# Hybrid pooling and stick-breaking trunk on one core: the z and gate strips of the input projection by seven block products instead of eight

## What is computed

```python
def reference(x, norm_g, w_in, b_gate, pool_w, pool_scale, w_pool_up, w_attn_up, w_out, final_g):
    ...
        h = rms_norm(x, norm_g[l])
        proj = jnp.einsum('bsd,de->bse', h, w_in[l])
        u_pool, z_pool, q, k, v, z_attn, gate_logits = jnp.split(proj, splits, axis=-1)
        y_pool = multiscale_pool(u_pool, pool_w[l], pool_scale[l]) * jax.nn.silu(z_pool)
        attn = stick_breaking_attention(...)
        y_attn = attn.reshape(B, S, ATTN_WIDTH) * jax.nn.silu(z_attn)
        gates = jax.nn.sigmoid(gate_logits + b_gate[l]).reshape(B, S, 2, D)
        merged = (gates[:, :, 0] * jnp.einsum('bsp,pd->bsd', y_pool, w_pool_up[l])
                  + gates[:, :, 1] * jnp.einsum('bsa,ad->bsd', y_attn, w_attn_up[l]))
        x = x + jnp.einsum('bsd,de->bse', merged, w_out[l])
    return rms_norm(x, final_g)
```

## Time and profile before

| | |
|---|---|
| three runs, median | 1686.95 us (1686.09 to 1690.57) |
| the profiled execution | 1688.91 us |
| its span (first to last instruction) | 1687.1 us |
| PE busy | 1649.3 us (98%), 8306 matmuls |
| DVE busy | 930.7 us (55%) |
| ACT busy | 689.8 us (41%) |
| POOL busy | 550.8 us (33%), 468 instructions |
| DMA | 170.16 MB, 31.9% of 16 engines |
| mean granted clock of PE | 0.995 |

### The profile page before, as it was taken

The page is one execution under the profiler, slowest core; times in us unless marked ns, Lnnn a source line. Parts: engine busy times, 40 slices in busy tenths (PEclk is TensorE's granted clock), DMA queues, the critical chain, the costliest instruction groups (busy, mean ns, idle before and its releaser), DMA issues. The chain is left out here.

```text
span 1687.1 us, 25908 instructions
## 1 busy us (share of the span) xinstructions
PE 1649.3 (98%) x8306; PEld 1374.1 (81%) x8306; DVE 930.7 (55%) x1311; ACT 689.8 (41%) x1335; POOL 550.8 (33%) x468
## 2 busy tenths in 40 slices
PE   8999999998999999999999999999999899999998
PEld 6878888886888888888878888888888678888886
DVE  6736410004776678766767666777666674333423
ACT  4422221114555565555545555655555441111111
POOL 3531111115343354342443433543411341414040
PEclk9999999999999999999999999999999999999999
DMA  7621131222332232222313322322213573535331
GB/s 251 230 102 50 63 106 69 75 90 72 101 94 63 67 88 85 73 76 70 95 51 99 94 64 67 88 83 74 76 54 119 178 234 121 153 112 162 112 99 75
DMA packets 119930, 170.16 MB, mean 101 GB/s; under 512 B 44401, under 2 KB 61297, under 8 KB 119810
## 3 DMA queue, kind: packets, MB, share of 16 engines
q1 hardware_dynamic: 119810, 168.68, 31.9%
HBM read 114.11 MB, written 54.53 MB: 100 GB/s over the span
## 5 line engine op out<-in xcount | busy, mean ns | idle before, releaser
L1295 DVE TENSOR_TENSOR_SCAN left<-keep,left 128x512 f32<-128x512 f32 x192 | 285.2, 1485 | 119.7 <-ACT keep L1199 96.4
L1091 PE MATMUL psum<-hT_hi,w_parts 128*128 128x512 f32 x760 | 312.5, 411 | 1.3 <-POOLq L1424 1.3
L1093 PE MATMUL psum<-hT_lo,w_parts 128*128 128x512 f32 x760 | 307.5, 405 | 0.0
L1095 PE MATMUL psum<-hT_hi,w_parts 128*128 128x512 f32 x760 | 307.0, 404 | 0.0
L1199 ACT ACTIVATE keep<-psum 128x512 f32<-128x512 f32 (+3 forms) x320 | 170.9, 534 | 233.7 <-PE psum L1110 231.2
L1292 DVE TENSOR_TENSOR_SCAN left<-keep,floor 128x512 f32<-128x512 f32 (+3 forms) x128 | 112.4, 878 | 224.6 <-ACT keep L1199 223.6
L1206 ACT ACTIVATE wt<-psum 128x512 fp32r<-128x512 f32 (+3 forms) x320 | 170.7, 533 | 159.6 <-PE psum L1119 157.0
L1347 POOL TENSOR_TENSOR y_out<-row_sum 64x128 f32<-64x128 f32 x128 | 76.5, 598 | 398.5 <-DVE row_sum L1311 393.0
L1301 DVE TENSOR_TENSOR wt<-psum,wt 128x512 fp32r<-128x512 f32 (+3 forms) x320 | 192.1, 600 | 21.3 <-ACT wt L1206 14.4
L1130 PEld LDWEIGHTS psum<-wt,vm 128*128 128x128 f32 x1088 | 169.6, 188 | 34.1 <-DVE wt L1301 6.9
L1130 PE MATMUL psum<-wt,vm 128*128 128x256 f32 x1088 | 182.5, 282 | 3.0 <-DVE wt L1301 2.8
(11 more groups left out here) (123 smaller groups left out, 2644.7 us busy)
## 6 DMA issues: line engine op xcount, KB each, us to landing
w_raw<-in_w_strips SPq DMA_DIRECT2D x36, 512.0 KB, 4.2
gate_scratch<-staging SPq DMA_DIRECT2D x64, 256.0 KB, 2.5
gate<-gate_scratch SPq DMA_DIRECT2D x64, 256.0 KB, 4.0
xt<-in_x SPq DMA_DIRECT2D x16, 512.0 KB, 5.1
xT<-in_x_T SPq DMA_DIRECT2D x16, 512.0 KB, 4.1
qk_scratch<-staging SPq DMA_DIRECT2D x32, 256.0 KB, 2.4
k_raw<-qk_scratch SPq DMA_DIRECT2D x64, 128.0 KB, 3.3
q_raw<-qk_scratch SPq DMA_DIRECT2D x128, 64.0 KB, 2.6
```

Source lines behind the costliest of these rows:

```text
L1091: pe.matmul(o, hi, hT_hi[:, kt, tok], start=kt == 0, stop=False)
L1093: pe.matmul(o, hi, hT_lo[:, kt, tok], start=False, stop=False)
L1095: last = pe.matmul(o, lo, hT_hi[:, kt, tok], start=False, stop=kt == KT - 1)
L1295: dve.tensor_tensor_scan(left[:, n % 4, span][:, ::-1], k, k, carry, ALU.mult, ALU.bypass).then_inc(scanned, 1)
```

## The change

Take two strips (rows A1, A2 of a 2x2 block matrix, with K cut in two halves of 512: A11, A12, A21, A22) and two chunks of tokens (B11, B12, B21, B22). Four strip products are eight products of blocks, 12 matmuls each. The change makes them from **seven** block products by sums of blocks (Winograd's form): S3 = A11 - A21, S2 = A22 - S3, S1 = S2 + A11, S4 = A12 - S2 of the weights, and T1 = B12 - B11, T3 = B22 - B12, T2 = B22 - T1, T4 = B21 - T2 of the tokens; the seven products are summed into four results.

- **Groups.** 24 groups of two strips by two chunks (1024 tokens), in two phases: first all strips for the first 1024 tokens, then all for the other 1024. Group 0 stays plain (4 strip products; the first of them is now strip z 0 by chunk 1, at the end of stage 2); the other 23 have 7 products of 12 matmuls. The filler of stage 3 goes from 95 x 24 = 2280 matmuls to 3 x 24 + 23 x 84 = 2004.
- **Weights.** For each group POOL forms four sums of blocks (128x512) and splits off seven low halves (128x512, `ring`, five places); ACT makes the seven high halves.
- **Sums of products.** For each group ACT copies two products from PSUM (`take`), DVE adds five (`add_part`, line 1581 of the changed kernel), POOL adds two pairs in SBUF (`join`). The z groups' product with the sigmoid (`silu`) now reads its strip from SBUF.
- **Token sums.** Eight (T1 to T4 for each phase, with their parts) are made in stage 2 by DVE (80 additions of 128x512), ACT (32 high parts) and POOL (32 low parts), and stored to DRAM (`form_d`); the first phase's are loaded at the end of stage 2 and the opening of stage 3, the second phase's, with B11, B21 and B22, as 28 DMAs of 512 KB around the middle of stage 3, one to a step.
- **Written out.** Stage 3's loop over the two middle pairs is gone: all 320 steps are written out on every engine. `hT` is one tensor by blocks. Some of stage 4's tiles lie elsewhere.

```diff
+HK = KT // 2
+FORMS = 7
+B11, B21, T2, T1, T3, B22, T4 = range(FORMS)
+A11, A12, S2, S1, S3, S4, A22 = range(FORMS)
+HOME = {B11: 0, B21: 1, B22: 3, T2: 4, T1: 5, T3: 6, T4: 7}
...
 # stage2, SP
+            def put_t(v):
+                f, kk, i = t_unit(v)
+                sp.wait_ge(t_lo_done, v + 1)
+                sp.dma_start(form_d[f, TURN[i], kk], t_parts[:, i, :, :].bitcast(F32)).then_inc(t_stored[i], DMA)
+            def load_t(j):
+                for kk in range(HK):
+                    sp.dma_start(hT[:, HOME[j], kk, :, :].bitcast(F32), form_d[0, j, kk]).then_inc(form_in[j], DMA)
...
 # stage2, DVE
+            for f in range(2):
+                b11, b21, b12, b22 = range(4 * f, 4 * f + 4)
+                for kk in range(HK):
...
+                    dve.tensor_tensor(t_rest[:, 0, :], lo[2], lo[0], ALU.subtract).then_inc(t_step, 1)
+                    dve.tensor_tensor(t_rest[:, 1, :], lo[3], lo[2], ALU.subtract).then_inc(t_step, 1)
+                    dve.tensor_tensor(t1, hi[2], hi[0], ALU.subtract).then_inc(t_step, 1)
...
 # stage3
-    STRIPS = 6
-    GROUPS = STRIPS * NC
-    MM = 3 * KT
+    GROUPS = 6 * PAIRS
+    MM = 3 * KT
+    PART = 3 * HK
+    PLAIN = 4
...
+    cost = [450.0 + 3.1 * item(n)[3] for n in range(ALL)]
+    SWITCH = part(GROUPS // 2 - 1, 0)
+    calm = range(ALL // 2 - 14, ALL // 2 + 18)
+    cost = [x * (0.8 if s in calm else 1.0) for s, x in enumerate(cost)]
...
+    AHEAD_OF = (3, 3, 4, 4, 5, 5, 5)
+    def split_step(w):
+        return max(fin[freed(w)], fin[PLAIN + w - AHEAD_OF[w % FORMS]]) + 1
...
 # stage3, PE
-        with eng.Fori(1, PAIRS - 1) as p:
-            walk(p, range(NI), True, True, True)
+            def form_part(g, j):
+                w = split(g, j)
...
+                pe.wait_ge(w_lo_done, w + 1)
+                if g == 1 and j in (T1, T2, T3, T4):
+                    pe.wait_ge(form_in[j], HK * DMA)
+                if g == GROUPS // 2:
+                    pe.wait_ge(form_in[j], (2 if j in (T1, T2, T3, T4) else 1) * HK * DMA)
...
 # stage3, ACT
+            def take(g, j):
...
+                act.activation((sum_a if j == A11 else sum_c)[:, :], bank_p(part(g, j)), ACT.Copy).then_inc(taken, 1)
...
 # stage3, DVE
+            def add_part(g, j):
+                dve.wait_ge(part_done, part(g, j) + 1)
...
+                elif j == S3:
+                    dve.wait_ge(joined, 2 * (g - 1) + 1)
+                    dve.wait_ge(summed, 5 * (g - 1) + 2)
...
+                dve.tensor_tensor(to[:, :], bank_p(part(g, j)), a[:, :], ALU.add).then_inc(summed, 1)
...
 # stage3, POOL
+            def low_w(w):
+                g, j = w // FORMS + 1, w % FORMS
+                if j == A11:
...
+                    step(blocks[S3][:, :, :], blocks[A11][:, :, :], blocks[S3][:, :, :], ALU.subtract,
+                         w_formed, 4 * (g - 1) + 1)
...
+                    step(blocks[S2][:, :, :], blocks[A22][:, :, :], blocks[S3][:, :, :], ALU.subtract,
+                         w_formed, 4 * (g - 1) + 2)
+                pool.wait_ge(w_hi_done, w + 1)
+                step(ring[:, w % RING, 1, :, :], blocks[j][:, :, :], ring[:, w % RING, 0, :, :].bitcast(F32),
+                     ALU.subtract, w_lo_done, w + 1)
+                if j == A11:
+                    step(blocks[S1][:, :, :], blocks[S2][:, :, :], blocks[A11][:, :, :], ALU.add,
+                         w_formed, 4 * (g - 1) + 3)
+                if j == A12:
+                    step(blocks[S4][:, :, :], blocks[A12][:, :, :], blocks[S2][:, :, :], ALU.subtract,
+                         w_formed, 4 * (g - 1) + 4)
+            def join(g, j):
+                if j == S1:
...
+                    step(sum_b[:, :], sum_a[:, :], sum_c[:, :], ALU.add, joined, 2 * (g - 1) + 1)
+                else:
+                    pool.wait_ge(summed, 5 * (g - 1) + 3)
+                    step(sum_c[:, :], sum_a[:, :], sum_c[:, :], ALU.add, joined, 2 * (g - 1) + 2)
```

More of the change, by code:

```diff
@@ new lines, in split, with kind, strip_of @@
+    def split(g, j):
+        return (g - 1) * FORMS + j
+    PARTS = part(GROUPS, 0)
+    size = [MM] * PLAIN + [PART] * (PARTS - PLAIN)
+    ends_at = [sum(size[1:r + 1]) for r in range(PARTS)]
+    TOTAL = ends_at[-1]
+    def kind(g):
+        return min(g % 6, 2)
+    def strip_of(g, a):
+        phase, q = divmod(g // 6, 2)
+        base = (S_ZP + 2 * q, S_ZA + 2 * q, S_G + 8 * q + 2 * (g % 6 - 2))[kind(g)]
+        return base + a
+    RESULTS = 4 * GROUPS
+    PLAIN_OUT, OUT = [(0, 1), (1, 1), (0, 0), (1, 0)], [(0, 0), (1, 1), (0, 1), (1, 0)]
@@ new lines, in stage3 @@
+    cost = [x * (0.8 if s in calm else 1.0) for s, x in enumerate(cost)]
+    KEPT, EARLY = MM, MM // 2
+    due, run = [], 0.0
+    for s in range(ALL):
+        run += cost[s]
+        n = round(run / sum(cost) * (TOTAL - KEPT))
+        due.append(max(n, min(MM, EARLY + 4 * (s + 1)), min(2 * MM, MM + 4 * (s - 1)), due[-1] if due else 0))
+    due += [TOTAL - KEPT + round((s + 1) / (AV_LAG + 1) * KEPT) for s in range(AV_LAG + 1)]
+    fin = [-1] + [next(s for s in range(len(due)) if due[s] >= ends_at[r]) for r in range(1, PARTS)]
@@ new lines, in at, with steps_of @@
+    def at(steps, s):
+        return [u for u, step in enumerate(steps) if step == s]
+    def steps_of(count, step):
+        return [step(u) for u in range(count)]
+    K_LOAD, V_LOAD, Q_LOAD = steps_of(PAIRS * NK, k_load), steps_of(PAIRS * NK, v_load), steps_of(PAIRS * NQ, q_load)
+    K_STEP, V_STEP, D_STEP = (steps_of(PAIRS * NK, f) for f in (k_step, v_step, d_step))
+    Q_STEP = steps_of(PAIRS * NQ, q_step)
+    W_STEP = steps_of(split(GROUPS, 0), split_step)
+    PART_END = [f + 1 for f in fin]
@@ new lines, in projections, with score @@
+            def projections():
+                for r in range(1, PLAIN):
+                    yield from plain_part(r)
+                for g in range(1, GROUPS):
+                    for j in range(FORMS):
+                        yield from form_part(g, j)
+            def score(n):
+                w = item(n)[3]
+                i, c = item(n)[1:3]
+                wait(pe, keep_done, n - 1)
+                pe.wait_ge(k_lo, key_unit(n) + 1)
+                u = query_unit(n)
+                pe.wait_ge(q_lo, u + 1)
@@ L1117, in turn @@
+                pe.matmul(bank_s(n)[:, 0:w], qm_lo[:, u % QN, cols], km[:, keys], start=False,
+                          stop=True).then_inc(scored, 1)
+            def turn(n):
+                w = item(n)[3]
+                pe.wait_ge(scanned, n + 1)
+                wait(pe, wt_lo_done, n - 1)
                 for j in range(w // P):
@@ L1167, in _ @@
-            running = [None]
-            turns(pe, walk)
+            pe.sem_inc(part_done, 1)
+            filler = projections()
+            done = 0
+            for done in range(1, EARLY + 1):
+                next(filler)
+            for s in range(len(due)):
+                middle = (due[s - 1] if s > 0 else 0) + due[s]
+                if s < ALL:
+                    score(s)
+                while 2 * done < middle:
+                    next(filler)
+                    done += 1
+                if 0 <= s - T_LAG < ALL:
+                    turn(s - T_LAG)
+                while done < due[s]:
+                    next(filler)
+                    done += 1
+                if 0 <= s - AV_LAG < ALL:
+                    weigh(s - AV_LAG)
@@ new lines, in _ @@
+            for s in range(-9, END):
+                for g in range(1, GROUPS):
+                    for j in (A11, S1):
+                        if s == PART_END[part(g, j)]:
+                            take(g, j)
+                if 0 <= s < ALL:
+                    remaining(s)
+                for u in at(K_STEP, s):
+                    split_k(u)
+                for u in at(V_STEP, s):
+                    split_v(u)
+                for u in at(Q_STEP, s):
+                    split_q(u)
+                for w in at(W_STEP, s):
+                    split_w(w)
+                if 0 <= s - T_LAG < ALL:
+                    high_part(s - T_LAG)
+                if s - AV_LAG - 1 in LAST:
+                    other_half(s - AV_LAG - 1)
+                for k in at(RESULT, s):
+                    result(k)
```

1165 lines of the change are left out of this document (622 added, 543 removed).

## The result

| | before | changed |
|---|---|---|
| median of four runs | 1687.9 us | 1765.5 us (1764.99 to 1765.54) |
| span of the profiled execution | 1687.1 | 1763.6 |
| PE busy | 1649.3 | 1629.8, 8030 matmuls |
| DVE, ACT, POOL busy | 930.7, 689.8, 550.8 | 1135.2, 787.7, 1016.7 |
| mean granted clock of PE | 0.995 | 0.971 |

The change makes the kernel slower: 1.0458 times the time of before (95% interval 1.0445 to 1.047), 78 us, where 17 were forecast and the range ended at 1745. One execution of a kernel further down (the spread one with reloaded weights) was disturbed: it took 2274 us at a mean clock of 0.65, and its median and ratio leave it out.

A forecast was written before the change was run, and what follows sets the result against it. PE bounds the kernel now; POOL was to become stage 3's bound. Stage 3 +9, stage 2 +2, opening +4, middle +2 on 1688.9 gave 1706, forecast as 1704 us because the profiled execution lies 2 above the median; range 1628 to 1745.

The forecast's parts named there:

- rival 1: Stage 3: PE stays the bound, POOL needs 784 us, stage 3 falls to 856, time 1626; chance 0.21.
- POOL becomes the bound: Stage 3: POOL needs 911 us with the scans in its way, more than PE's 862.
- 1 us a group, 23 us (ends 0 and 69): Stage 3: allowance for POOL falling behind at each group's start and holding up `y_out` and `joined`.
- 596 us of POOL's own work: Stage 3: POOL's 213 us of kept work plus 383 us for 299 new instructions of 128x512.
- 225 of the scans' hold: Stage 3: POOL held 215 us by scans and 10 by z products; ends 98 and 258.
- 654 of 934, hidden: Stage 3, ACT: high halves and copies add under 143 us, busy 654 of 934, so no time added.
- Rival 3: Stage 3: each group's crowd stops PE 3 us and lowers its clock; stage 3 1005, time 1775; chance 0.08.
- Rival 2: Stage 3: POOL and scans exclude each other for whole instructions; 959 us that can't overlap, time 1729; chance 0.10.
- The opening, 4 us (ends 0 and 12): Start of stage 3: eight 512 KB loads ahead of the last v rows take 12 us; 4 us added.
- Stage 2 (+2): Stage 2: making the token sums on DVE, POOL and ACT adds 2 us; ends 0 and 14.
- the middle (+2): Middle of stage 3: 28 loads of 512 KB, hidden but for the last, add 2 us; ends 0 and 10.
- DVE at most 848: Stage 3: DVE busy at most 848 of 934 us, 91%, nearly full but not the bound by itself.

The follow-up runs named there:

- the spread one with reloaded weights: The spread kernel with the second half's split weight parts stored earlier and loaded from DRAM, not formed again: 1697.9 us, ratio 1.0052.
- The spread kernel: Changed kernel with form loads spread, POOL's v difference two steps earlier, and its eleven weight operations of a group one to a step: 1733.7 us, ratio 1.0266.
- the twins: Two versions of the kernel before with 256 unread POOL subtractions added, spread evenly or in crowds: 1713.0 and 1809.8 us.
- the earlier v: Changed kernel with the eight T3 and T4 loads moved, plus POOL's v difference and its load two steps earlier: 1751.0 us.
- the even twin: Kernel before with 256 unread POOL subtractions of 128x512, one in four steps of five: 1713.0 us, ratio 1.0146.
- the crowded twin: Kernel before with 256 unread POOL subtractions, 64 to a pair, in crowds of four, three, one, one and one: 1809.8 us, ratio 1.072.

## Why the prediction was wrong

- **Slower, and through POOL's new work: right.** PE ceased to be the bound, the 63 us of filler came off it and were overpaid. With POOL's work short the kernel is at 1659, on the way to rival 1's 1626.
- **The failed step: "POOL becomes the bound", with only "1 us a group, 23 us (ends 0 and 69)" for engines that wait for each other.** The forecast's stage 3 is 596 us of POOL's own work, 90 of gaps, 225 of the scans' hold and these 23. The changed kernel's rows, with the same 596, give a hold of 777.5 - 596 = 181, gaps of 73, and 147 us in which POOL is idle, over twice the upper end of 69: 997 in all. So the hold was 44 us too large: POOL is busy 777.5 where 820 were forecast, the `ring` subtractions have a median of 1.30 us, not "well above 1.28", and the scans a mean of 1.59 where 1.7 was forecast. What was missing is waiting, 124 us more than forecast, 16 us of the 147 in the opening (before 430) and 80 at `y_out` for `row_sum`. The spread kernel says the same: 596 + 184 + 75 + 112 = 967 of its 969. POOL with its gaps fills 85% of stage 3; it delays the others without being full.
- **The way was wrong too.** The prediction let POOL's lag arrive at DVE's `row_sum`, which waited 9 us. It came by ACT, which was costed as a sum of busy time, "654 of 934, hidden": ACT was busy 590, but its queue is in order, and one `split_v` or `split_w` that waits for POOL stops `keep` and `wt` behind it, so DVE and PE. In the twins the place alone is worth 97 us at equal amounts; in the changed kernel itself spreading and the earlier v gave 17 + 5.5, close to the 23 us that the prediction had for crowds, but this was not all of the waiting.
- **Rival 3, PE's clock: had the mechanism and the number**, 1005 us for stage 3 and 1775 in all against 998 and 1765.5. Its price of 23 stops of 3 us was, by the timeline, 14 of 2 us and more with 45 us together, besides many short ones, and 40 us of slow clock. I gave it 0.08 because POOL's lag would reach PE "through buffers, in small pieces"; between POOL's `v_raw` and ACT's next instruction there is none. Crowding and clock should not have been two cases either: the first causes the second.
- **Rival 2 (1729)** has the time of the kernel with the crowds spread (1733.7), but that is luck: its 959 us that can't overlap took 870, and for the other 99 us of stage 3 neither POOL nor a scan or z product ran.
- **The opening, 4 us (ends 0 and 12): too small.** PE was busy 15.04 us of 35 against 29.88, 15 us less, and the clock at 0.80. Moving the loads gave 9 back. Not bytes alone were late: SP's issues stood in line, a mixer tile landed 5 us after its issue, and ACT waited 16.3 us for the first block, with `keep` behind it.
- **Stage 2 (+2), the middle (+2), stages 1 and 4 (0), DVE at most 848 and not the bound: right.** Stage 2 took 3 more, PE's waits for the reloaded forms were 3.3 us, DVE printed 769 and twice did not matter.

Not settled: how much of the 46 us by which the spread kernel is over the one before comes from the hold between POOL and the scans and how much from the order of the queues. No run had POOL's operations without that hold. The twins can't tell either: the even twin's 945 us are mostly PE, busy in 918 of them.

## What to carry to other kernels

Work that is moved to an idle engine costs by where it stands too, not only by its share: count how many microseconds of it lie in one piece ahead of a small operation that another engine waits for at the head of its queue, and follow that wait to the engine that sets the pace. If the piece is longer than the slack of that chain, spread it over the steps before adding anything, and look at the time in which POOL or a scan runs (89% in the changed kernel) before believing either engine's row. In a forecast, an engine at 85% of a stage is no bound yet: what it and the others wait for each other needs a term of its own, here 147 us and the largest error. Removing the longest wait in the list moved it; making the work less (here once instead of twice) gained more than spreading it.

## What the hardware showed that was not expected

- Equal additional work on POOL, 256 subtractions of 1.04 us, cost 25 us evenly spread and 122 in crowds of four, three and one.
- PE's clock is part of the price of stops: after one of 5.55 us matmuls printed 0.63 instead of 0.40 us for 5 us, and 13 of the 14 stops of 2 us and more in the changed kernel were followed by the lower clock, in the spread kernel 6 of 10. Over stage 3 that made 40 us in the changed kernel and 41 in the crowded twin, a third of its loss; the even twin, whose longest stop for `wt` was 1.3 us, kept 1.00.
- A scan with both inputs in SBUF and POOL's subtractions slow each other almost by their whole length (2.35 us for 1.27, 4.18 for 2.56) where they meet, though over the whole stage some 90 of 959 us overlapped. DVE's additions with an input in PSUM don't suffer (670 to 692 ns), and shortening them gave 2 us of 1734.
- A subtraction of 128x512 on POOL whose two inputs are one tile printed 1.04 us, with two tiles 1.26.
- Storing and reloading the weights raised the traffic from 229 to 298 MB, in stage 3 from 105 to 190 GB/s; it cost nothing that these runs show, as long as no load stood behind a wait on SP's queue; where one did, PE stopped for 8 us.
